# A two-layer hybrid step: expert results scattered to token rows, the second attention's front in another order

## The reference, cut to what matters

```python
    a = jnp.einsum('td,edf->tef', x, w_gate)
    up = jnp.einsum('td,edf->tef', x, w_up)
    mid = jax.nn.silu(a) * up * gates[:, :, None]
    y = jnp.einsum('tef,efd->td', mid, w_down)
```

## Time and profile before

| | us |
|---|---|
| median of 3 runs (945.0 to 947.19) | 946.19 |
| the profiled execution's own time | 944.43 |
| its span | 942.6 |
| PE busy, 85% | 801.3 |
| DVE busy, 40% | 378.5 |
| ACT busy, 29% | 271.2 |
| POOL busy, 10% | 96.6 |
| DMA moved | 226.45 MB |
| mean granted TensorE clock | 0.925 of full |

### The profile page before, as it was taken

The page is one execution under the profiler, slowest core; times in us unless marked ns, Lnnn a source line. Parts: engine busy times, 40 slices in busy tenths (PEclk is TensorE's granted clock), DMA queues, the critical chain, the costliest instruction groups (busy, mean ns, idle before and its releaser), DMA issues.

```text
span 942.6 us, 11489 instructions
## 1 busy us (share of the span) xinstructions
PE 801.3 (85%) x4035; PEld 442.6 (47%) x4035; DVE 378.5 (40%) x844; ACT 271.2 (29%) x631; POOL 96.6 (10%) x146
## 2 busy tenths in 40 slices
PE   4779999999888998999871779888799989999760
PEld 0237665635443456555430445555454565555330
DVE  3375583355154341422113434664651433322114
ACT  1241111210541242222212326565530432222111
POOL 3200000001000012000004002212200031000002
PEclk9879999999989996999996779999999978999995
DMA  9991155369972276999997927202109379999965
GB/s 287 368 339 48 48 144 164 102 208 352 263 291 89 90 244 248 361 410 410 410 347 249 382 99 263 90 2 91 47 20 367 125 269 324 401 410 412 399 235 200
DMA packets 85055, 226.45 MB, mean 240 GB/s; under 512 B 8596, under 2 KB 18509, under 8 KB 84681
## 3 DMA queue, kind: packets, MB, share of 16 engines
q1 hardware_dynamic: 72706, 193.89, 56.8%
q0 software_dynamic: 8576, 21.62, 7.3%
q10 hardware_dynamic: 3720, 10.25, 2.9%
HBM read 216.60 MB, written 17.78 MB: 249 GB/s over the span
## 4 chain that ended last, share of the span: by engine, by line
PE 65%; DMA 12%; DVE 8%; issue 6%; ACT 3%; SPq 3%; DVEq 2%; POOLq 0%; POOL 0%; ACTq 0%
PE ps L876 58%; PE ps L883 4%; DMA ring<-in_moe_w_up_dram 4%; DMA arena<-in_moe_w_up_dram 3%; DMA ring<-in_w_mod_dram 2%; PE ps L1103 2%; DVEq L1849 2%; SPq L638 1%; DMA arena<-y_rows,rows_out 1%; DVE negmax L1902 1%; SPq L655 1%; DMA hT<-h_rows,rows_in 1%; ACT hT L1564 1%; DVE xn L2293 1%; DMA hT<-mod_rows 1%
## 5 line engine op out<-in xcount | busy, mean ns | idle before, releaser
L876 PE MATMUL ps<-arena 128*64 128x256 f32 (+12 forms) x1164 | 243.1, 457 | 25.9 <-DMA arena<-in_moe_w_up_dram 7.9
L876 PEld LDWEIGHTS ps<-arena 128*64 128x64 f32 (+4 forms) x1164 | 131.9, 172 | 119.5 <-issue 69.1
L876 PE MATMUL ps<-ring,hT 128*128 128x512 f32 (+2 forms) x384 | 134.0, 509 | 6.5 <-issue 5.9
L876 PE MATMUL ps<-ring,arena 128*64 128x256 f32 (+1 forms) x784 | 111.3, 431 | 6.8 <-DMA ring<-in_moe_w_down_dram 3.3
L876 PEld LDWEIGHTS ps<-ring,hT 128*128 128x128 f32 x384 | 73.3, 192 | 65.1 <-issue 60.8
L876 PEld LDWEIGHTS ps<-ring,arena 128*64 128x64 f32 x784 | 53.8, 137 | 52.9 <-issue 30.4
L883 PE MATMUL ps<-ident,arena 128*128 128x128 f32 (+2 forms) x332 | 51.1, 294 | 20.8 <-DVE hT L1908 5.6
L1521 ACT ACTIVATE arena<-ps 128x256 f32<-128x256 f32 (+5 forms) x88 | 38.7, 454 | 94.8 <-PE ps L876 88.2
L2233 DVE TENSOR_TENSOR arena<-arena,ps 128x128 f32<-128x128 f32 x37 | 10.7, 288 | 130.9 <-ACT arena L1626 130.9
L876 PE MATMUL ps<-hT,ring 128*128 128x384 f32 x192 | 62.1, 486 | 0.0
L876 PE MATMUL ps<-ring,condT 128*32 128x512 f32 x384 | 54.2, 692 | 7.4 <-DMA ring<-in_w_mod_dram 6.8
(11 more groups left out here) (295 smaller groups left out, 842.2 us busy)
## 6 DMA issues: line engine op xcount, KB each, us to landing
ring<-in_w_mod_dram SPq DMA_DIRECT2D x48, 1024.0 KB, 9.5
ring<-in_moe_w_down_dram SPq DMA_DIRECT2D x22, 1024.0 KB, 17.4
ring<-in_moe_w_gate_dram SPq DMA_DIRECT2D x38, 512.0 KB, 13.7
ring<-in_moe_w_up_dram SPq DMA_DIRECT2D x38, 512.0 KB, 15.7
arena<-in_moe_w_gate_dram SPq DMA_DIRECT2D x36, 512.0 KB, 9.0
arena<-in_moe_w_up_dram SPq DMA_DIRECT2D x36, 512.0 KB, 10.8
arena<-in_moe_w_down_dram SPq DMA_DIRECT2D x15, 1024.0 KB, 12.1
ring<-in_ev_w_in_dram SPq DMA_DIRECT2D x9, 1024.0 KB, 13.0
```

Of the source, the lines that this page charges most:

```text
L876: mm = pe.matmul(out, lhsT, rhs, **kw)
```

## The change

1. `y_rows` now has a row for each token and choice (2 x 384) and no zero tail. The index product makes two lists: the rows to gather, and the rows to write to. The eight stores by ScalarE become eight indirect scatters by POOL, which drop unused slots; an overflow block's store becomes a scatter too, with a list that VectorE copies ahead of its result copy.
2. The read-back is six plain loads, three of ScalarE's queue (first choice) and three of SP's (second).
3. POOL gathers the first looped overflow block ahead of the loop, between the scatters of pairs 6 and 7.
4. Behind layer 0's experts TensorE runs 28 products of constants into a free bank.
5. ScalarE modulates all of tile 0; VectorE's call for it goes.
6. The latents are normed in two parts, tiles 0 and 1, then 2; TensorE transposes in the order 0, 1, cached, 2, and the projection waits for tile 2 only before its own tile 2.

```diff
+LATENT_ORDER = (0, 1, 3, 2)
...
-    c["ids"] = np.arange(T).reshape(NT, P).T - NO_ROW
+    token = np.arange(T).reshape(NT, P).T - NO_ROW
+    c["ids"] = np.concatenate([token, token, token, token + T], 1)
...
-        rows_in = ctx.enter_context(nc.sbuf_tensor("rows_in", [P, NPAIR], mybir.dt.int32))
+        rows_in = ctx.enter_context(nc.sbuf_tensor("rows_in", [P, 2 * NPAIR], mybir.dt.int32))
...
-        y_rows = nc.dram_tensor("y_rows", [NROWS, D], F32, kind="Internal").ap()
+        y_rows = nc.dram_tensor("y_rows", [2 * T, D], F32, kind="Internal").ap()
...
+            def rows_back(l, nb):
+                sp.wait_ge(y_stored[0][l], 16 * (NPAIR // 2))
+                sp.wait_ge(y_stored[1][l], 16 * (NPAIR // 2 - 1))
+                sp.wait_ge(over_stored[l], nb * 16 + 16)
+                for t in range(NT):
+                    sp.dma_start(y_of[1][:, t, :], y_rows[T + P * t:T + P * t + P, :]).then_inc(y_back[t], 16)
...
-                    send_over(0)
+                    nb = send_over(0)
...
+                    rows_back(0, nb)
...
-            send_over(1)
+            rows_back(1, send_over(1))
...
-            pool.dma_start(y_rows[NMAIN:NROWS, :], d["zero_row"].partition_broadcast(NROWS - NMAIN)).then_inc(rows_zeroed, 16)
...
+                def scatter(c):
+                    for half in range(2):
+                        pool.wait_ge(y_read[half][l], 2 * c + 2)
+                    pool.indirect_dma_start(y_rows, bass.IndirectOffsetOnAxis(ap=rows_in[:, NPAIR + c:NPAIR + c + 1], axis=0), ysb[:, c % 2, :], None,
+                                            bounds_check=2 * T - 1, oob_is_err=False).then_inc(over_stored[l] if c == NPAIR - 1 else y_stored[c % 2][l], 16)
+
+                for c in range(3):
+                    scatter(c)
...
                 pool.wait_ge(over_rows[l], 1)
                 pool.wait_ge(xt_full[1][l], 3)
                 pool.indirect_dma_start(xg_over, None, h_rows[l], bass.IndirectOffsetOnAxis(ap=rows_over[:, 0:1], axis=0), bounds_check=T - 1, oob_is_err=False).then_inc(
                     over_gathered[l], 16)
+                for c in range(3, NPAIR - 1):
+                    scatter(c)
+                pool.wait_ge(row_ready[l], 1)
+                pool.wait_ge(xt_full[1][l], NPAIR + 1)
+                pool.indirect_dma_start(xg_over, None, h_rows[l], bass.IndirectOffsetOnAxis(ap=row_now[:, :], axis=0), bounds_check=T - 1, oob_is_err=False).then_inc(
+                    over_gathered[l], 16)
+                scatter(NPAIR - 1)
...
                 with pool.Fori(0, nb) as b:
-                    pool.wait_ge(row_ready[l], b + 1)
-                    pool.wait_ge(xt_full[1][l], b + (NPAIR + 1))
-                    pool.tensor_tensor(pool_mark[:, :], pool_mark[:, :], pool_mark[:, :], ALU.mult)
+                    pool.wait_ge(row_ready[l], b + 2)
+                    pool.wait_ge(xt_full[1][l], b + (NPAIR + 2))
+                    pool.tensor_tensor(pool_mark[:, 0:1], pool_mark[:, 0:1], pool_mark[:, 0:1], ALU.mult)
                     pool.indirect_dma_start(xg_over, None, h_rows[l], bass.IndirectOffsetOnAxis(ap=row_now[:, :], axis=0), bounds_check=T - 1, oob_is_err=False).then_inc(
                         over_gathered[l], 16)
                     pool.drain()
+                    pool.wait_ge(over_done[l], b + 2)
+                    pool.wait_ge(y_read[1][l], b + (NE + 1))
+                    pool.tensor_tensor(pool_mark[:, 1:2], pool_mark[:, 1:2], pool_mark[:, 1:2], ALU.mult)
+                    pool.indirect_dma_start(y_rows, bass.IndirectOffsetOnAxis(ap=to_now[0:HALF, :], axis=0), ysb[0:HALF, 0, :], None,
+                                            bounds_check=2 * T - 1, oob_is_err=False).then_inc(over_stored[l], 16)
                 pool.wait_ge(over_stored[l], nb * 16 + 16)
-                pool.tensor_tensor(pool_mark[:, :], pool_mark[:, :], pool_mark[:, :], ALU.mult)
+                pool.tensor_tensor(pool_mark[:, 0:1], pool_mark[:, 0:1], pool_mark[:, 0:1], ALU.mult)
                 pool.drain()
-                for c in range(2):
-                    pool.wait_ge(y_stored[c][l], 16 * (NPAIR // 2))
-                for t in range(NT):
-                    for s in range(2):
-                        pool.indirect_dma_start(y_of[s][:, t, :], None, y_rows, bass.IndirectOffsetOnAxis(ap=rows_out[:, 2 * t + s:2 * t + s + 1], axis=0)).then_inc(
-                            y_back[t], 16)
...
+            for half in range(2):
+                pe.wait_ge(y_read[half][0], NE)
+            for _ in range(28):
+                product(ps[Y_BANKS[1]][:, 0:2 * P], ident[:, :], rowsel[:, :, :].rearrange("p a b -> p (a b)"), start=True, stop=True)
             mixer_turn(1, 0)
             latent_in(0)
...
-            pe.wait_ge(lora_ready, NT)
             loaded(pe, in_mla)
-            for t in range(NT + 1):
+            for t in LATENT_ORDER:
+                pe.wait_ge(lora_ready, t + 1 if t == 2 else 2)
                 bank = claim("cT", t)
...
-            for t in range(NT + 1):
+            for t in LATENT_ORDER[:-1]:
...
+                    if g == 0 and t == NT - 1:
+                        drained_wait(pe, "cT", t)
...
-                def store(c):
-                    for half in range(2):
-                        act.wait_ge(y_read[half][l], 2 * c + 2)
-                    act.dma_start(y_rows[P * c:P * c + P, :], ysb[:, c % 2, :]).then_inc(y_stored[c % 2][l], 16)
...
-                    act.wait_ge(over_done[l], b + 2)
-                    act.wait_ge(y_read[1][l], b + (NE + 1))
-                    act.dma_start(y_rows[bass.ds(b * HALF + NMAIN, HALF), :], ysb[0:HALF, 0, :]).then_inc(over_stored[l], 16)
+                act.wait_ge(y_stored[1][l], 16 * (NPAIR // 2 - 1))
+                act.wait_ge(over_gathered[l], nb * 16 + 32)
+                act.wait_ge(over_stored[l], nb * 16 + 16)
+                for t in range(NT):
+                    act.dma_start(y_of[0][:, t, :], y_rows[P * t:P * t + P, :]).then_inc(y_back[t], 16)
...
-            modulate_tile(1, 0, 0, "hT1.0", 0)
+            for half in range(2):
+                modulate_tile(1, 0, 0, "hT1.0", half, 4 * half)
...
-            ins.then_inc(lora_sq, 1)
-            act.wait_ge(lora_var, 1)
-            act.activation(statA[:, 1, 0:2 * NT], statA[:, 0, 0:2 * NT], ACT.Sqrt).then_inc(lora_root, 1)
-            for t in range(NT + 1):
+                if t:
+                    ins.then_inc(lora_sq, 1)
+                    act.wait_ge(lora_var, t)
+                    act.activation(lora_part(1, t), lora_part(0, t), ACT.Sqrt).then_inc(lora_root, 1)
+            for t in LATENT_ORDER:
...
-                dve.tensor_tensor(tabs, tabs, ids[:, :].unsqueeze(1).unsqueeze(3).broadcast_to([P, 2, NT, NPAIR]), ALU.mult)
+                dve.tensor_tensor(row_table[:, 0:4 * NT * NPAIR].rearrange("p (i k c) -> p k i c", k=2, c=NPAIR), by(pair_ids, NPAIR).unsqueeze(1).broadcast_to([P, 2, 2 * NT, NPAIR]),
+                                  ids[:, :, :].unsqueeze(3).broadcast_to([P, 2, 2 * NT, NPAIR]), ALU.mult)
                 dve.drain().then_inc(hit_ready, 1)
                 bank = filled_wait(dve, f"idx{l}")
-                drain_inc(dve.tensor_scalar(rows_in[:, :], bank[:, 0:NPAIR], float(NO_ROW), None, ALU.add), f"idx{l}")
+                drain_inc(dve.tensor_scalar(rows_in[:, :], bank[:, 0:2 * NPAIR], float(NO_ROW), None, ALU.add), f"idx{l}")
...
+                    dve.tensor_copy(to_now[0:HALF, :], rows_to[0:HALF, bass.ds(b, 1)])
+                    settle()
...
-            modulate_tile(1, 0, 0, "hT1.0", 1)
...
+            for last in (1, 2):
+                dve.wait_ge(lora_sq, last)
+                var, root = lora_part(0, last), lora_part(1, last)
+                dve.tensor_scalar(var[:, 0, :], var[:, 0, :], 1.0 / QR, EPS, ALU.mult, ALU.add)
+                dve.tensor_scalar(var[:, 1, :], var[:, 1, :], 1.0 / KVR, EPS, ALU.mult, ALU.add)
+                dve.drain().then_inc(lora_var, 1)
+                dve.wait_ge(lora_root, last)
+                dve.reciprocal(root, root)
+                settle()
+                for t in (0, 1) if last == 1 else (2,):
+                    for c0, c1, i in ((0, QR, t), (QR, QR + KVR, NT + t)):
+                        ins = dve.scalar_tensor_tensor(out=um[:, t, c0:c1], in0=um[:, t, c0:c1], scalar=statA[:, 1, i:i + 1],
+                                                       in1=lgain[:, c0:c1], op0=ALU.mult, op1=ALU.mult)
+                    ins.then_inc(lora_ready, 1)
```

49 lines of the change are left out of this document (18 added, 31 removed).

## The result

The changed kernel took 938.31 us (median of 7 runs, 931.05 to 939.94), the kernel before 946.19 us beside it (7 runs, 940.98 to 948.47): ratio 0.9888, 95% interval 0.985 to 0.9925. So it is faster, by 1.1%. The profiled execution took 938.66 us with a span of 936.8, 5.8 less than before.

The account below looks back on a forecast made before the run. TensorE was taken as the bound, 65% of the chain of work that ended last. Terms 2.6 + 2.4 + 1.9 + 0 + 4.1 + 3.7 - 0.4 = 14.3 us gave 930.1 profiled, 931.9 on the median; range 925.0 to 939.0.

Parts of the forecast that it names:

- one sign of being wrong: End of the expert stage: result copies waiting for the scatters would show the forecast wrong.
- Read-back: End of each layer's experts: scatter and plain loads replace store and gathers, 1.3 us gained per layer, 2.6 in all.
- Stores in the expert stage: Second half of each expert stage: scatters drop empty slots and relieve full DMA engines, 1.2 us per layer, 2.4 in all.
- Tile 0's modulation: Ahead of tile 0's projection: ScalarE does all eight modulations instead of waiting for VectorE's half, 1.9 us gained.
- Constant products: TensorE behind layer 0's experts: 28 products delay nothing, and the clock is low again at tile 0's projection; counted 0.
- The rival by which they hold the clock: Constants keep TensorE's clock full up to tile 0's projection: gains 2.0 us, 929.9; chance 0.15.
- Latents in two parts: Front of the second layer's attention: tiles 0 and 1 normed while tile 2 is projected; next projection starts 4.1 us earlier.
- Head projection at full clock: Projection behind the latents: its 20 matmuls take 4.8 us instead of 8.47, 3.7 us gained.
- The rival that the clock falls between the early transposes and the projection: Front of the second attention: short transposes do not hold the clock; costs the 3.7 us, 935.6; chance 0.20.
- Planning: Making the lists of rows: index product twice the columns, table twice the elements; 0.2 us lost per layer, -0.4.
- What the front gains is passed on: Second layer's attention behind the front: its DMA engines wait for free ring slots, so the front's gain is kept.
- Scatters that hold the result buffers: Expert stage: rival that late scatters delay result copies beyond 17.2 us; at 22 us 28.8 lost, 960.7; chance 0.03.

Follow-up runs that it names:

- experiment 4: Changed kernel with POOL's drain moved ahead of the overflow gather and constant products in the gaps (36, 7 and 4): 933.54 us, 0.9855 of the kernel before.

## Why the prediction was right, and where not

The forecast was 931.9 us, the measurement 938.31, within the range but near its upper end: 7.9 us of 14.3 gained. By the ratios of its two measurements (0.9888 and 0.986), 946.19 becomes 935.6 and 932.9. Direction and mechanism held in the main. The eight stretches of the table gave 13.2 us of 14.7, and this is closer than the terms deserve: the read-back gave 1.3 more than forecast and the head projection 2.3 less. Of the signs named, three came true (tile 0 scaled 9.6 us after the last result; the projection 3 us after the first modulation, at half clock; the next projection within 4 us), one did not (20 matmuls under 5.5 us at full clock), the scatter landed sooner than the 3 to 4.5 us given, and one sign of being wrong appeared: the last result copy waits for a scatter. Point by point:

- **Read-back, 2.6 forecast, 3.9 measured** (2.0 and 1.9; over all fourteen profiles the stretch splits cleanly, 9.4 to 9.7 us in the eleven with it, 11.4 to 11.8 in the three without). The mis-sized term is the scatter's landing: I took 3.6 us "nearest to the gather", it is 2.58 and 2.55. The plain store of the same block, 3.0, had been the better row. I had also sized it by a full block, and left out here that a scatter drops the empty slots: from 503.1 to 505.7 POOL's queue moved 0.09 MB, a third of what the store moved before (queue, packets, MB, share; the change, then before):

```profile
q0 software_dynamic: 80, 0.09, 16.1%
...
q10 hardware_dynamic: 80, 0.26, 41.2%
```

The loads took 5.2 us from issue to scaling, 4.7 forecast. The Trainium skill, "DMA: Bandwidth & Descriptors", section "Anatomy of one DMA — SWDGE (gpsimd) path", gave 2.6 us for a full block, near to the 2.58 of this trace, and I had let the gather's 4.46 speak against it. But by the bytes that moved its rule gives an estimated 2.2 us, 0.4 less than measured, so the near hit on 2.6 is chance. Under load the scatter took 6.36.
- **Stores in the expert stage, 2.4 forecast, 2.1 in the profiled pair** (2.4 in layer 1, -0.3 in layer 0), but by two steps that I didn't have as they are. The dropped rows are shown as a relief in layer 0 alone: once the drain is gone, writing them again costs 2.1 us there. With the drain in place the stage's median in layer 0 is what it was (127.4 after 127.3), without it 126.0. In layer 1 the medians fell from 137.9 to 135.8, but the dropped rows aren't shown to be the reason: writing them again cost nothing there, and one of the three profiles with stores, 136.7, lies among those with scatters. What failed is "Scatters also sit in POOL's order ahead of the overflow gathers ... nothing": I looked at the gathers that come behind scatters, and not at the scatter behind a gather and its drain, nor at the last copy that waits for it. The new wait is 1.6 to 2.7 us long in five kernels of five, of which 1.4 us counted.
- **Tile 0's modulation, 1.9: measured 1.9.**
- **Constant products, 0: measured 0.** They hid wholly and bought nothing. The clock fell 5 us behind them, as it had 5 us behind the last product before, and rose 4 us after the projection's start, 0.2 later than before. The 5 us from which I argued are of one profile; in the twelve profiles in which it fell behind the last product or the constants, it did so after 2.3 to 5.3 us. The rival by which they hold the clock fell, because one gap stayed open ahead of the transposes (8.87 us) and one behind them. Filled too, as in experiment 4, they bring that rival's 2.0 and more: 19.63 us for the three projections against 21.05 to 22.45.
- **Latents in two parts, 4.1: measured 4.0**, 4.3 in most of the others.
- **Head projection at full clock, 3.7: measured 1.4.** The rival that the clock falls between the early transposes and the projection came true in the profiled execution, at the price of 1.3 us against the full clock, not 3.7. Two sizes were off. At full clock the 20 matmuls take 5.7 us, not 4.8, so the whole term is 2.7: the 28 of the earlier trace rows are not "of the same kind", but 20 like these, which took 5.6 us (578.65 to 584.25), and 8 narrower ones, and a row prints the shape of its first only. And at the fall the clock came back after 3.4 us, where it had stayed low for 10.2 before. "The longest gap is now about 2 us, less than either time after which it fell" was no bound: it fell with a gap of 2.3 us in five kernels of seven, and in the second profile of the kernel before it fell 2.25 us behind the last product.
- **Planning, -0.4: measured 0 to -0.1.** From the table's product to the list of rows it was 3.40 us (358.31 to 361.71) and is 3.18 in layer 0. In layer 1, from there to the first gather, it was 4.42 and 4.43 us in the two profiles of the kernel before and is 4.48 and 4.47 in the two of the changed one. The list's 4.4 us of delay in the profiled pair were there before this point or come of the wait for `h_rows`.
- **"What the front gains is passed on" held on the mean**: the second attention behind it takes 210.1, 213.3 and 210.4 us with the old front and between 208.9 and 214.5, 211.6 in the mean, with the new.
- **Scatters that hold the result buffers**: no copy of the main part waited for one. They land in 7.5 us where the stores took 7.1 (medians; 8.9 at most in the profiled execution), far from the 17.2 that they have.

Left open: whether the first gather of layer 0 comes later by the change. It came at 364.2 to 368.7 in the eleven profiles with scatters, and at 362.8, 364.7 and 366.3 in the three without. In ten of the fourteen, one of those without among them, it left 4.6 to 4.9 us behind the landing of the last `h_rows` store, for which POOL waits with a drain behind; in the four others 1.1 to 1.5 us behind the list of rows. So that landing, at 357.4 to 364.1, is what moves. I made no run that holds it still. Untested as well is the simplest cure for the new wait: to leave out the gathers that fetch no row.

## What to carry to other kernels

A drain is harmless only as long as nothing urgent is issued behind it on its engine: when a transfer is moved to an engine's queue, read every wait and drain of its program that now stands ahead of it, and who waits for the transfer. Ask of a loop that fetches ahead what its last passes fetch, and who waits for that. To keep TensorE's clock up, filler products have to stand in each gap ahead of the work that is to run fast; one block of them ahead of two gaps bought nothing here. And where single executions spread by as much as the effect, compare the stretches that the edit touches over several profiles, and take the others for what they are.
